# Moving the low halves of three operand pairs to the remainder (by 256 bytes) of their high halves

## The reference, cut to what matters

```
h = rmsnorm(x, norm_mix);  proj = h @ w_in
... mixers ...
x = x + merged @ w_mix_o
h = rmsnorm(x, norm_ffn)
gt, up = split(h @ w_ffn_in)
x = x + (silu(gt) * up) @ w_ffn_out
```

## Time and profile before

| | |
|---|---|
| median of three runs | 2160.33 us (2158.07 to 2161.37) |
| profiled execution, its own time | 2157.08 us |
| its span, first to last instruction | 2155.2 us |
| TensorE busy | 2131.1 us (99%), 18740 matmuls |
| VectorE, ScalarE, GpSimd busy | 1639.8, 1215.0 and 54.7 us |
| mean granted TensorE clock | 0.999 |
| DMA | 175 GB/s over the span |

### The profile page before, as it was taken

One profiled execution on the slowest core, in us unless ns is written; L12 is line 12 of the kernel. 1 busy time (PEld: TensorE's weight loads), 2 busy tenths in 40 slices (PEclk: granted clock), 3 DMA queues, 4 the chain that ended last, 5 costly groups with the idle time before them and its releaser, 6 DMA issues.

```text
span 2155.2 us, 47946 instructions
## 1 busy us (share of the span) xinstructions
PE 2131.1 (99%) x18740; PEld 2073.5 (96%) x18740; DVE 1639.8 (76%) x2627; ACT 1215.0 (56%) x1825; POOL 54.7 (3%) x53
## 2 busy tenths in 40 slices
PE   9999999999999999999999999999999999999998
PEld 8999999999999999899999999999899999999998
DVE  8997877987678766788947877766678947877774
ACT  6656544556656445446658845445446658845444
POOL 0000000000000000000002200000000002200000
PEclk9999999999999999999999999999999999999999
DMA  6444655644456556554544456556554544465553
GB/s 249 157 135 151 205 186 185 201 153 147 138 167 219 188 188 210 170 169 142 176 157 154 150 193 208 186 188 211 173 166 147 174 159 147 149 195 186 186 191 130
DMA packets 102976, 376.54 MB, mean 175 GB/s; under 512 B 11680, under 2 KB 11808, under 8 KB 102304
## 3 DMA queue, kind: packets, MB, share of 16 engines
q1 hardware_dynamic: 101664, 368.66, 51.9%
q10 hardware_dynamic: 1152, 5.58, 0.7%
HBM read 373.14 MB, written 1.05 MB: 174 GB/s over the span
## 4 chain that ended last, share of the span: by engine, by line
PE 90%; DVE 6%; ACT 2%; issue 1%; DMA 0%; DVEq 0%; ACTq 0%
PE acc L764 25%; PE acc L766 24%; PE acc L765 24%; DVE w_lo L1799 2%; PE acc L883 1%; PE acc L885 1%; PE acc L884 1%; PE acc L828 1%; PE acc L830 1%; PE acc L829 1%; ACT w_hi L1317 1%; PE mid L1120 1%; PE mid L1219 1%; DVE pr L2558 0%; PE mid L951 0%
## 5 line engine op out<-in xcount | busy, mean ns | idle before, releaser
L1799 DVE TENSOR_TENSOR w_lo<-w_raw,w_hi 128x1024 fp32r<-128x1024 f32 x694 | 847.7, 1226 | 321.8 <-ACT w_hi L1317 313.6
L1317 ACT CAST w_hi<-w_raw 128x1024 fp32r<-128x1024 f32 x694 | 723.8, 1046 | 542.2 <-PE acc L766 480.8
L764 PE MATMUL acc<-h_hi,w_hi 128*128 128x256 f32 x2096 | 599.7, 286 | 0.1
L765 PE MATMUL acc<-h_lo,w_hi 128*128 128x256 f32 x2096 | 588.9, 281 | 0.0
L766 PE MATMUL acc<-h_hi,w_lo 128*128 128x256 f32 x2096 | 585.7, 279 | 0.0
L764 PE MATMUL acc<-g_hi,w_hi 128*128 128x256 f32 x1456 | 412.3, 283 | 0.8 <-DVE w_lo L1799 0.7
L765 PE MATMUL acc<-g_lo,w_hi 128*128 128x256 f32 x1456 | 407.7, 280 | 0.0
L766 PE MATMUL acc<-g_hi,w_lo 128*128 128x256 f32 x1456 | 407.4, 280 | 0.0
L764 PEld LDWEIGHTS acc<-h_hi,w_hi 128*128 128x128 f32 x2096 | 393.7, 188 | 6.3 <-issue 5.0
L765 PEld LDWEIGHTS acc<-h_lo,w_hi 128*128 128x128 f32 x2096 | 395.3, 189 | 0.5
L766 PEld LDWEIGHTS acc<-h_hi,w_lo 128*128 128x128 f32 x2096 | 395.6, 189 | 0.0
(11 more groups left out here) (444 smaller groups left out, 3450.0 us busy)
## 6 DMA issues: line engine op xcount, KB each, us to landing
w_raw<-weights_d SPq DMA_DIRECT2D x695, 512.0 KB, 3.6
p<-p_d ACTq DMA_DIRECT2D x3, 1080.0 KB, 8.3
rdec<-decay_d ACTq DMA_DIRECT2D x2, 768.0 KB, 5.0
p<-p_d SPq DMA_DIRECT2D x1, 1024.0 KB, 10.7
out_d<-work SPq DMA_DIRECT2D x4, 256.0 KB, 2.4
x_all<-x_d SPq DMA_DIRECT2D x1, 516.0 KB, 4.5
w_raw<-weights_d SPq DMA_DIRECT2D x2, 256.0 KB, 5.8
x_all<-x_d SPq DMA_DIRECT2D x1, 512.0 KB, 6.2
```

The costliest lines, as they stand in the source:

```text
L764: mm(dst, wh, hi[:, k, :], start=first and j == 0, stop=False)
L765: mm(dst, wh, lo[:, k, :], start=False, stop=False)
L1317: nc.scalar.copy(w_hi[:, slot, :], w_raw[:, slot, :]).then_inc(hi_done, 1)
L1799: tt(w_lo[:, slot, :], w_raw[:, slot, :], w_hi[:, slot, :].bitcast(F32), SUB).then_inc(lo_v, 1)
```

## The change

The three low halves are placed so that their distance to the high half is a multiple of 1024 bytes. `h_lo` moves down by 32 bytes to data address 82192 (remainder 16, that of `h_hi`); `work`, behind it, stays where it was. `f_lo` moves down by 64 bytes to 140272 (remainder 240, that of `f_hi`). `g_lo` moves down by 128 bytes to 178224 (remainder 48, that of `g_hi`). No instruction, semaphore or order differs; the addresses inside the instructions do.

```diff
         h_hi = place("h_hi", [P, KD, T], F32R, x_at + 4 * KD * T, lead=4)
-        top[0] += 4 * (2 * KD * T + 8)
-        h_lo = place("h_lo", [P, KD, T], F32R, lead=4)
+        h_lo = place("h_lo", [P, KD, T], F32R, x_at + 8 * KD * T, lead=4)
+        top[0] += 4 * (3 * KD * T + 16)
         work_at = top[0]
@@
         f_hi = in_arena("f_hi", 0, [P, FF, T], F32R, lead=4)
-        f_lo = in_arena("f_lo", 22592, [P, FF, T], F32R, lead=4)
+        f_lo = in_arena("f_lo", 4 * FF * T, [P, FF, T], F32R, lead=4)
         f_act = in_arena("f_act", 46144, [P, 2, T])
         f_prod = in_arena("f_prod", 48192, [P, 2, T])
         g_hi = in_arena("g_hi", 52288, [P, KD, T], F32R, lead=4)
-        g_lo = in_arena("g_lo", 60608, [P, KD, T], F32R, lead=4)
+        g_lo = in_arena("g_lo", 52288 + 4 * KD * T, [P, KD, T], F32R, lead=4)
```

## The result

The change made the kernel slower: 2162.44 us (median of 22 runs, 2159.7 to 2164.36) against 2158.57 us (22 runs, 2155.76 to 2161.37). The ratio is 1.0017 with a 95% interval of 1.0011 to 1.0023, so 3.9 us, or 2.4 to 5.0. More runs of before also moved the level that the forecast started from: the median of three was 2160.33 us, that of 22 is 2158.57.

What follows compares the result with a forecast made beforehand. The prediction took TensorE's pace from matmul to matmul as the bound. Its terms, -2.0 (h) + 0 (g) + 0 (f) + 0 (VectorE) = -2.0 us, took 2160.3 to 2158.3 us, range 2155.0 to 2163.5.

Steps and rivals of the forecast that it cites:

- What bounds the kernel: TensorE, busy 2131.1 of 2155.2 us with hardly any waits; the change can act only through the matmuls' pace.
- h: 6432 matmuls reading h lose the 0.31 ns excess of halves 32 bytes off: 2.0 us less (bounds 3.2 less, nothing).
- g: 4368 matmuls reading g, already at the level of m and o: 0, with an upper end of 3.9 us more.
- The other end of the term: Matmuls of g at the 118.7 ns of L805 and L806, 0.9 ns above g's pace: 3.9 us more.
- The two reasons for 0: For g: instruction order is m's, not L805's; and low halves meet `w_hi` only from remainders high halves already use.
- f: 2112 matmuls reading f, already at 117.78 ns: 0, with ends of 1.9 us more and 0.4 us less.
- VectorE: Writes of the low halves change by at most 7 ns each, 1.4 us in all, hidden under TensorE: 0.
- g gets slower: Feed-forward input pace goes to 118.7 ns, +3.9 us; with h's gain 2162.2 us; chance 0.17.
- the 8.6 ns: Gap between the measured 117.78 ns per matmul and the skill page's 109.2; some 110 us if from badly placed halves; no chance.
- the short row: Earlier-trace runs on one high half: L805/L806 on `g_hi`, 118.7 ns over 30 intervals; L777/L778 on `h_hi`, 117.6 over 29.

Runs made afterwards that it cites:

- h alone: Only the h edit (`h_lo` moved) on the kernel before: 2158.03 us, ratio 0.9998 (0.9989 to 1.0007).
- the map: Kernel of its own, TensorE only, 318 sets of remainders, including all 256 high/low pairs with weights at 176 and 240: paces between 115.6 and 120.1 ns.
- g alone: Only the g edit (`g_lo` moved) on the kernel before: 2163.68 us, ratio 1.0024 (1.0014 to 1.0034).
- f alone: Only the f edit (`f_lo` moved) on the kernel before: 2159.45 us, ratio 1.0009 (1.0000 to 1.0018).
- the busy kernel: Only the three `products` lines over 38 remainder sets, with VectorE, ScalarE and DMA traffic beside; all sets within 0.12 ns of the same kernel without traffic.
- the pair kernel: Kernel of its own repeating one weight block and one moving block 48 times for each of 74 address pairs; the pace repeated every 256 bytes of distance.

## Why the prediction was wrong

**What bounds the kernel.** Right: no wait and no other engine took part in the difference, and it is all in the pace.

**h.** Right in size: the two stretches were forecast at 50.76 us and took 50.77. Over all intervals that begin in a matmul of h, the edit was worth 1.5 us in the profile of h alone, for a forecast of 2.0. The reason given, that the halves lay 32 bytes apart, was not the cause as such: in the map, (16, 128) with unlike halves ran at 116.7 ns, faster than (16, 16) with 117.9. L781, on `h_lo` alone, was named as a place to see a remainder act by itself and does not show it: its two runs took 0.84 and 1.02 us for 7 intervals before and with h alone, but 0.83 and 0.98 with g alone, where `h_lo` had not moved.

**g.** This is the step that failed: "I take 0, as the order of the instructions is that of m, not that of L805; this is the least certain term." The other end of the term, 3.9 us from the earlier trace rows, was the truth, and slightly low: g's pace rose by 1.1 ns, and over all intervals that begin in a matmul of g that was 4.6 us. L809, on `g_lo` alone, rose with it, by 1.3 ns over five of its runs, and by 0.9 with g alone; L805 and L806 kept their pace, as the text said they must. The two reasons for 0 were both wrong. That m and o run at 117.78 ns with equal halves says nothing about halves at 48, since the pace depends on the distance to the weights (48 from `w_hi` for them, 128 here). And "no new pair of a moving and a stationary remainder arises" looked at single matmuls: in g's own row the low half at 176 stood between two high ones at 48, and that order kept the one pace at all 16 starts, while 48, 48, 48 has a slow pattern., where every moving operand began at 48, were the nearest thing to it, at 118.7 ns over 30 intervals. That `g_lo` moved makes g slow is shown by g alone; why all its stages took the slow one of two patterns is not known.

**f and VectorE.** f: 0 was right in three of four stages, and the first lost 0.3 us by a switch of pattern. The price of up to 1.9 us that the text gave for f at the pace of the earlier trace rows is nearly what f alone then showed (1.1 ns on the 1563 intervals of its three later stages is 1.7 us). VectorE: right, the write of `f_lo` still takes 426 ns.

**The sum.** -1.5 + 4.6 + 0.3 is 3.4 us, within the measured 2.4 to 5.0. The case was in the text as the rival "g gets slower", with a chance of 0.17, and its mechanism came true. That its 2162.2 us lie so near the measured 2162.44 is luck: the rival was worth 1.9 us on top of 2160.33, and the change was worth 3.9 on top of 2158.57. The forecast pointed the other way because the term with the largest range was set to its lower end.

**The cited rules.** The one from the Trainium skill on the pace (TensorE: Matmul & The Clock Gate, section "Wait — 56ns, not 53.3ns?"), an estimate of 109.2 ns by its figure, was met by none of the runs (113.3 ns was the lowest pace). I argued from m and o, whose halves agree, that badly placed halves could not explain the 8.6 ns. That was right of halves that differ and wrong of places: those to the weights explain half of it, as 117.78 fell to 113.4. "PE and ACT never wait on anyone" (the Trainium skill, SBUF — State Buffer, section "Who interferes with whom") agrees with the busy kernel as far as the other engines go; what the prediction drew from it, that no place of an operand changes a pace, does not hold here. That TensorE's two own reads, weights and moving operand, hold each other up is my reading of the pair kernel and the map, where nothing else ran, and no run looks inside it.

## What to carry to other kernels

When TensorE is busy nearly all the time, compute its pace from long stretches, and compare tiles: a difference of 0.3 ns that repeats from stretch to stretch is worth a search for its cause. Where an operand's place is changed, think of its distance to all that is read beside it, the weights above all, and look for a row in which every operand already lies as it will; such a row, even a short one, marks an end of the range to be taken seriously. For g the short row said 118.7 ns and 118.9 came; for h it said 117.6 and 117.8 came, the level of the long rows, so a short row is no more than that. A small kernel that only issues the matmuls over many distances costs one run; it was this that led to the 46 us.

## What the runs showed of the hardware

- Matmuls of 256 columns with a weight load beside each ran at 113.3 to 120.1 ns at full clock, by the places of their operands (all starting on a 16-byte line) and what ran before. For one repeated pair the pace repeats with every 256 bytes of distance; 112 and 192 were the best. The place by itself matters too: 16 bytes turned 114 into 119.9 ns at distance 112.
- 117.8 ns (within 0.12) is the pace of 86 of the 256 sets in the map with the weights at 176 and 240 (47 intervals each), over unlike distances. All of them lie between 115.6 and 120.1.
- The same instructions at the same addresses can hold two paces, 117.8 or 118.9 ns, for a whole stage of 60 us; with one weight tile moved, 115.6 or 118.9. The pace changed at a gap of 0.43 us between two starts in one kernel (not in another), and with what ran before the stage.
- Moved by 4 and 8 bytes against a 16-byte line, one pair ran at 123.1 and 126.6 ns, moved by 12 at 116.7.
